# Projection steps between the levels of the inverse and the blocks of attention, 20 per pair, instead of in the chain of states

## The reference

```python
xn = rms_norm(h, norm1_g)
proj = xn @ w_in       # q, k, v, dn_qkv, z, b, a, gate_sb, gate_dn
o_sb = stick_breaking_attention(pad4(q), pad4(k), pad4(v), key_valid)
qkv = silu(causal_depthwise_conv(dn_qkv, dn_conv_w))
o_dn = gated_delta_rule_chunked(dq, dk, dv, beta, g)      # per chunk: t_inv = (I + M)^-1, then a scan over states
o_dn = rms_norm(o_dn) * silu(dn_z)
mix = sigmoid(gate_sb) * (o_sb @ w_sb_out) + sigmoid(gate_dn) * (o_dn @ w_dn_out)
h = h + mix @ w_o
h = h + peer_ffn(rms_norm(h, norm2_g), ...)
```

## Time and profile before

| | us |
|---|---|
| median of 3 runs | 2159.39 |
| lowest and highest | 2157.39, 2159.63 |
| the profiled execution | 2157.28 |
| its span in the trace | 2155.5 |
| front: four pairs | 90 to 724 |
| TensorE busy in the span | 1984.9 (92%) |
| VectorE, ScalarE, GpSimd busy | 1391.9, 817.5, 668.0 |

### The profile page before, as it was taken

The page is one execution under the profiler, slowest core; times in us unless marked ns, Lnnn a source line. Parts: engine busy times, 40 slices in busy tenths (PEclk is TensorE's granted clock), DMA queues, the critical chain, the costliest instruction groups (busy, mean ns, idle before and its releaser), DMA issues. The chain is left out here.

```text
span 2155.5 us, 30502 instructions
## 1 busy us (share of the span) xinstructions
PE 1984.9 (92%) x11569; PEld 1760.5 (82%) x11569; DVE 1391.9 (65%) x2636; ACT 817.5 (38%) x1260; POOL 668.0 (31%) x685
## 2 busy tenths in 40 slices
PE   7988988988988699999898999998989999999999
PEld 7765765765755587888898998998989999999999
DVE  5542442442442365379998968878857777777777
ACT  4333433433433343233333335665623333333332
POOL 4133033033022010037888781222212222222221
PEclk9999999999999899999999999999999999999999
DMA  3210210210210452236898886988879999899997
GB/s 117 78 40 1 74 40 1 74 40 1 74 45 1 162 178 98 88 120 232 277 334 270 301 278 210 329 332 304 310 257 327 330 322 328 304 322 328 328 323 251
DMA packets 153377, 421.75 MB, mean 196 GB/s; under 512 B 15760, under 2 KB 69136, under 8 KB 152592
## 3 DMA queue, kind: packets, MB, share of 16 engines
q1 hardware_dynamic: 114448, 279.27, 37.5%
q0 software_dynamic: 38784, 140.53, 19.8%
HBM read 365.21 MB, written 54.53 MB: 195 GB/s over the span
## 5 line engine op out<-in xcount | busy, mean ns | idle before, releaser
L1392 ACT ACTIVATE expert_hi<-raw 128x1024 fp32r<-128x1024 f32 x288 | 305.5, 1061 | 435.0 <-PE psE L86 378.8
L84 PE MATMUL psE<-x2h,expert_hi 128*128 128x384 f32 x1024 | 354.3, 346 | 29.9 <-POOL expert_lo L1511 19.1
L84 PE MATMUL psE<-w_hi,expert_hi 128*128 128x384 f32 x1024 | 352.7, 344 | 13.4 <-DVE w_lo L1753 6.2
L1547 DVE TENSOR_TENSOR expert_lo<-raw,expert_hi 128x1024 fp32r<-128x1024 f32 x212 | 259.3, 1224 | 150.1 <-ACT expert_hi L1392 149.2
L86 PE MATMUL psE<-x2h,expert_lo 128*128 128x384 f32 x1024 | 348.6, 340 | 0.0
L85 PE MATMUL psE<-x2l,expert_hi 128*128 128x384 f32 x1024 | 348.2, 340 | 0.0
L86 PE MATMUL psE<-w_hi,expert_lo 128*128 128x384 f32 x1024 | 344.8, 337 | 0.0
L85 PE MATMUL psE<-w_lo,expert_hi 128*128 128x384 f32 x1024 | 344.5, 336 | 0.0
L1505 POOL DMA_INDIRECT few_gathered<-in_peer_v,picked_expert x128 | 134.9, 1054 | 433.6 <-DVE shared L1719 388.1
L1511 POOL TENSOR_TENSOR expert_lo<-raw,expert_hi 128x1024 fp32r<-128x1024 f32 x76 | 195.6, 2574 | 144.6 <-ACT expert_hi L1392 143.0
L84 PEld LDWEIGHTS psE<-x2h,expert_hi 128*128 128x128 f32 x1024 | 197.3, 193 | 34.7 <-POOL expert_lo L1511 23.4
(11 more groups left out here) (286 smaller groups left out, 3629.9 us busy)
## 6 DMA issues: line engine op xcount, KB each, us to landing
raw<-in_peer_u SPq DMA_DIRECT2D x128, 512.0 KB
raw<-in_peer_v SPq DMA_DIRECT2D x128, 512.0 KB
expert_acts<-gelu SPq DMA_DIRECT2D x128, 192.0 KB
shared<-expert_acts SPq DMA_DIRECT2D x128, 192.0 KB, 3.3
expert_gates<-shared SPq DMA_DIRECT2D x5, 4096.0 KB, 16.3
shared<-expert_gates SPq DMA_DIRECT2D x32, 640.0 KB, 6.8
ring<-in_w_xonly SPq DMA_DIRECT2D x24, 512.0 KB, 3.3
ring<-in_w_full SPq DMA_DIRECT2D x16, 512.0 KB, 3.9
```

Source lines behind the costliest of these rows:

```text
L84: nc.tensor.matmul(out, sh, mh, start=first, stop=False)
L1392: nc.scalar.activation(wh[:, s % R, :], raw[:, s % R, :], ACT.Copy).then_inc(S["hi_done"], 1)
L1547: v.tensor_tensor(wl[:, s % R, :], raw[:, s % R, :], wh[:, s % R, :].bitcast(F32), ALU.subtract).then_inc(S["lo_done"], 1)
```

## The change

`room` gets a place inside each level, with room for two steps, and one step behind each `cum` unit that a `z` follows. On TensorE the steps of a level are issued between its second and its third tile. The casts of the level's place stand on ScalarE behind the level's copies, takes and subtractions on VectorE at the level's unit (where VectorE has no other work). Everything else, the quota and the places of the chain included, is as before; steps that find a place earlier are missing from the chain later.

```diff
         room += [(("kk", n), 2) for n in range(NT + 1)] + [("inverse0", 4)]
-        room += [(("unit", u), 0) for u in range(len(UNITS))] + [("wt", 4)]
+        for u, (unit, a) in enumerate(UNITS):
+
+            room += [(("level", a), 2)] if unit == "level" else []
+            room += [(("unit", u), 1 if unit == "cum" and UNITS[u + 1][0] == "z" else 0)]
+        room += [("wt", 4)]
         room += [(("chain", n, s), 4) for n in range(NT + 1) for s in range(2)] + [("end", 4)]
...
                             inc(nc.scalar.activation(ys[0:r, n, :, 0:r], bank[0:r, y_bank(t), 0:2 * r].rearrange(
                                 "p (e c) -> p e c", e=2), ACT.Copy), "y_copied")
+                        split("level", a)
...
+                    elif unit == "level":
+                        at("level", a)
                     elif unit == "soft":
...
                             inc(last, "y_ready")
+                            if n == tiles[1]:
+                                fill("level", a)
```

## The result

The changed kernel takes 2119.2 us (median of 4 runs, 2116.5 to 2122.7) beside 2159.5 before on the same chip: ratio 0.9819, interval 0.9803 to 0.9836, 40 us or 1.8% faster. Two more sets of runs on other occasions gave 0.9841 (0.9814 to 0.9868; 2123.5 us) and 0.9847 (0.9827 to 0.9868; 2123.2 us), 33 to 35 us. The profiled execution of the changed kernel took 2122.7, the slowest of its four runs, with a span of 2121.0 against 2155.5.

What follows compares the result with a forecast made beforehand. TensorE was taken as nearest to the bound, with unfilled waits in the levels and an overfilled chain. 3 x (12.1 - 7.3) + 4.9 = 19.3 us off 2157.3 gives 2138.0, median 2139; range 2122 to 2149.

Steps and rivals of the forecast that it cites:

- The chain: Chain of states, pairs 0 to 2: emptied of most steps, it and its tail save 12.1 us per pair.
- the tail: Last output matmul to sum of squares: from 3.26 us to 1.90, saving 1.4 per pair.
- the stretch ahead: L1130 to first state matmul, pairs 0 to 2: 8 steps before and after, 8.8 us, no change.
- The levels: Inverse's levels and attention, pairs 0 to 2: steps not fully hidden in gaps, 7.3 us added per pair.
- singles: Eight single steps between cum and z of attention blocks: 6.0 us into gaps of 4.3, cost 1.7 per pair.
- The waits for takes: TensorE waits for VectorE's takes before steps in levels 1, 3 and 5: 0.6, 2.2 and 1.4 us.
- Pair 3: Last pair, only 8 steps move: 5.65 us saved ahead of the first state matmul, 0.7 added, net 4.9.
- The clock: TensorE's granted clock: filled level gaps against bare chain ends, set at 0, between -1.5 and +1.5 us per pair.
- The upper rival: Takes in the levels don't delay TensorE and the clock gains 1.5 us per pair: 2122 to 2125; chance 0.18.
- Rivals two to four: Gain nearly eaten by ScalarE's casts (2149), clock loss (2148), steps not hidden (2179); chances 0.08 plus 0.04, 0.05, 0.05.
- rival three: One more 1.2 GHz stretch per pair and slow next start, 3 to 3.5 us: 2148; chance 0.05.
- slower: Level waits restart behind the steps, 19.2 us added per pair against 12.1 back: 2179; chance 0.05.

Runs made afterwards that it cites:

- take_first: Changed kernel with VectorE's take at units 17 and 33 put ahead of the subtraction of the split of units 16 and 32: 2111.0 us, ratio 0.9789.
- warm_end: Changed kernel plus two steps' worth of unread matmuls between a pair's last output matmul and its sum of squares: 2127.0 us, ratio 0.9871.
- idle_work_in_levels: Kernel before, nothing moved, plus 17 steps' worth of unread matmuls per pair in levels 2 to 6 and behind cums: 2159.7 us, ratio 1.0016.
- three_pairs: Changed kernel with no room in pair 3's levels and units, its 8 steps back at wt and in the chain: 2128.9 us, ratio 0.9869.
- singles_only: Changed kernel without the pairs of steps in the levels, keeping the 8 single steps behind cum units: 2137.9 us, ratio 0.9908.
- the fastest kernel: Changed kernel with VectorE's takes at units 0, 17 and 33 all ahead of the subtraction of the split before them: 2111.1 us, ratio 0.9782.

## Why the prediction was wrong

The sign, the places and the waits came as forecast; the size didn't. Of the 40.3 us of the first set 25.2 are the work that was forecast at 19.3, 5.3 are the clock that was put at 0, and 9.8 lie outside the four pairs or between executions, for which the range had no room. With the four pairs' 30.3 alone the time would have been 2129, inside the range.

**The chain: right, a little small.** Forecast 12.1 us per pair, measured 32.09 - 19.11 = 13.0. From first state matmul to last output matmul 9.1 was forecast and 9.04 measured, the tail 1.90 and 1.89. What was short is the stretch ahead, L1130 to the first state matmul: no change forecast, less 0.6 measured (8.81 to 8.18): the idle time of 0.49 us for the state in front of the first state matmul is gone, since four steps now stand there.

**The levels: right in kind, some terms too dear.** Forecast 7.3 added per pair; measured with the clock's falls set aside 55.01 - 50.5 + 1.87 = 6.4 (50.5 is 51.91 less one fall of 1.41; 1.87 is what the rest grew by). By level, from the starts of the third tiles and the scores: level 1 0.93 (forecast 0.8), level 2 0.01 (0), level 3 2.54 (3.1), level 4 0.10 (0.4), level 5 0.84 (1.5), level 6 1.12 (0.9), singles 1.1 (1.7). The waits for takes came where they were named, 0.76, 1.60 and 0.73 us. Levels 3 and 5 were too dear by one term: the subtraction was set at 1.75 us after the one row at 296.96, and took 1.22 here. In the trace before every other subtraction from 80 us on took 1.20 to 1.23; 1.75 stands only at this place, once in each of pairs 0 to 2. That GpSimd's masks beside it are the reason, as the prediction has it, isn't shown: in level 3 after, the masks run from 320.43 to 324.26, beside the whole subtraction, and it took 1.22. take_first shows that the order on VectorE was the cause of the waits.

**Pair 3: the work right, the rest missing.** Forecast 4.9 of work; measured 5.8 from the chain less 0.4 for the levels, 5.4.

**The clock: the step of the reasoning that failed.** "I set one against the other: 0" is wrong in size and also in how it was counted. One fall per pair was seen in the levels, with one slice as its row, though the windows on the levels at hand show 0.97, 0.97, 0.94 and 0.94: six falls, 8.5 us, of which five went. Put against it was a fall at each new bare end. That didn't come: in pair 1 the clock is 1.00 to the chain's end and through the eight steps behind it, and the sum of squares took 1.13 us (391.91) where 1.86 was feared. What came is one more fall each in the starts of pairs 1 and 2, 1.7 us in the four starts, and warm_end shows that the bare end doesn't make it; what does stays open. Net of the two 5.3 us in this pair of traces; over three traces of each kernel the front gained 28.5, which leaves 3.3 beside the same 25.2 of work. Sum: work 3 x (13.0 - 6.4) + 5.4 = 25.2 instead of 19.3, clock 5.3 instead of 0, together 30.5 against 30.3 measured in the front.

idle_work_in_levels shows that filled gaps alone take the falls out of the levels; in three_pairs and singles_only some come back without the doubles. The upper rival had this mechanism, with "the clock gains 1.5"; it was made to hang on the takes not biting, while they bit and the clock gained all the same.

The rule of the Trainium skill in "Perfetto Trace Analysis" (Matmul Optimizations), that matmuls belong back to back in batches, was weighed against the change. In these traces it speaks for it: the chain's clock was 1.00 before, dense, and 1.00 after, nearly bare, the levels were where TensorE paused, and bursts of one and two steps there kept its clock. How the falls spread over starts and levels isn't settled: they moved from one to the other between kernels and between executions of one kernel (changed kernel, pair 1: start 47.5 and levels 55.0 in one trace, 44.9 and 56.3 in another).

**The rest of the 40 us, and the range.** 30.3 us are the front in the first two traces, 4.4 the `back`, and 5.8 lie between executions: the one profiled before was 2.2 under its median, the one profiled after 3.5 above. Over three traces of each kernel the front is 627.4 against 598.9, 28.5, and `back` 1431.9 against 1430.6, scattering by 10 us whatever the kernel. The three sets of runs say 40, 35 and 33; the intervals of the two later ones reach down to 28.5, that of the first, 35.4 to 42.5, doesn't. The traces of the kernel before are all of executions at the fast end (each at or below the lowest time of its set), so they may understate the gain; the first set's excess has no cause shown. With the range's lower end at 2122 no room was left for such scatter: the three runs at hand lay within 2.3 us, where thirty-five runs of the kernel before, made on one later occasion, lie between 2148.6 and 2164.3.

**Rivals two to four** didn't come as such; of rival three half did, the slower start of the next pair, while the levels lost falls instead of gaining one. The y copies and exponentials are not waited for at all after the change, so the waits didn't restart behind the steps, and slower needed 12.1 us added where there were 6.4.

## What to carry to other kernels

Independent work belongs where the engine waits for another, not where it merely fits: read the idle time ahead of each group, put in pieces of the size of the gap, and look at what the piece itself must wait for on another engine's queue; here the order of take and subtraction on VectorE was worth 12 us of the fastest kernel's 45, 7.7 to 10.2 of them in the stretches where the waits stood. Where a stretch has short pauses, read its granted clock in windows for every repetition of the loop before costing a fill at the pauses alone; here it was worth 3 to 5 us beside 25. But fill with work that has to be done: unread work brought the clock of the levels to 1.00 and the kernel no time. And take the scatter of the untouched part from more than three runs before setting a range.

## What the runs showed that was not expected

With 78 more matmuls in them, the levels of pairs 2 and 3 ran in 52.3 us instead of 53.3, because the clock stayed at 2.4 GHz: TensorE did more in less time there, though the kernel as a whole gained nothing. A fall of the clock has nearly the same price wherever two traces or pairs with the same work in the levels differ by one, 1.25 to 1.43 us, and the starts of pairs 0 to 2 of the changed kernel take 44.9, 46.4 or 47.5 to 47.7 us at 1.00, 0.96 and 0.93 for the same work. A bare chain that ran at 1.2 GHz nearly throughout (0.60 in the mean) took 14.4 us instead of 10.9.
